# A hybrid encoder trunk: convolutions earlier into six buffers, the recurrence's odd blocks one slot later, and zero-padded keys in layer 0

## The reference

```
def bidirectional_rglru(xc, w_r, b_r, w_i, b_i, lam):
    ...
    r = jax.nn.sigmoid(jnp.einsum('bsne,dnef->dbsnf', xb, w_r...) + b_r...)
    i = jax.nn.sigmoid(jnp.einsum('bsne,dnef->dbsnf', xb, w_i...) + b_i...)
    log_a = -RG_C * r * jax.nn.softplus(-lam...)
    a = jnp.exp(log_a)
    u = jnp.sqrt(jnp.maximum(-jnp.expm1(2.0 * log_a), 0.0)) * (i * xf[None])
    h_fwd = linear_scan(a[0], u[0], reverse=False)
    h_bwd = linear_scan(a[1], u[1], reverse=True)
    return h_fwd + h_bwd

def even_mixer(h, ...):
    z = h @ w_in
    gate, xr, q, k, v = ...
    xc = lax.conv_general_dilated(xr, conv_w[:, None, :], ...) + conv_b
    y_a = bidirectional_rglru(xc, ...) * jax.nn.gelu(gate)
    y_b = dilated_mixture_attention(q, k, v).reshape(bsz, seq, B_WIDTH)
    return jnp.concatenate([y_a, y_b], axis=-1) @ w_out
```

## Time and profile before

| | |
|---|---|
| median of 3 runs | 2328.31 us (2327.73 to 2328.93) |
| the profiled execution: its own time | 2329.11 us |
| its span in the profile | 2327.3 us |
| PE busy in the span | 2273.3 us, 98% |
| DVE, ACT, POOL busy | 56%, 44%, 11% |
| mean granted clock of PE | 0.993 of full speed |

### The profile page before, as it was taken

The page is one execution under the profiler, slowest core; times in us unless marked ns, Lnnn a source line. Parts: engine busy times, 40 slices in busy tenths (PEclk is TensorE's granted clock), DMA queues, the critical chain, the costliest instruction groups (busy, mean ns, idle before and its releaser), DMA issues.

```text
span 2327.3 us, 27257 instructions
## 1 busy us (share of the span) xinstructions
PE 2273.3 (98%) x10273; PEld 1858.9 (80%) x10273; DVE 1313.6 (56%) x1308; ACT 1033.7 (44%) x1131; POOL 253.3 (11%) x243
## 2 busy tenths in 40 slices
PE   8989999899999999999999999999999999999997
PEld 6877778688888888888777777887888888888886
DVE  4567466654555555554655555676545555555555
ACT  5676444533333333343455555545434333333432
POOL 2463001400000000000340111014000000000002
PEclk9999999999999999999999999999999999999999
DMA  8545344555555555555454444555556555555552
GB/s 277 168 139 168 124 165 153 205 185 188 192 195 184 197 183 197 183 196 191 152 182 153 155 162 144 199 167 187 189 183 196 190 188 193 185 197 182 196 187 102
DMA packets 212263, 417.87 MB, mean 180 GB/s; under 512 B 12040, under 2 KB 12640, under 8 KB 211296
## 3 DMA queue, kind: packets, MB, share of 16 engines
q1 hardware_dynamic: 212192, 416.92, 54.3%
HBM read 414.79 MB, written 2.10 MB: 179 GB/s over the span
## 4 chain that ended last, share of the span: by engine, by line
issue 71%; PE 20%; POOL 4%; DVE 3%; DMA 1%; ACT 1%; SPq 0%; POOLq 0%; DVEq 0%; ACTq 0%
PE acc L937 16%; POOL yacc L1372 1%; PE tp L951 1%; DVE xs L1126 1%; DVE w_lo L1097 1%; PE sc L1018 1%; DMA gq<-in_norm_ffn_post 1%; POOL stage L1387 0%; PE sc L1023 0%; POOL small L1364 0%; PE sc L996 0%; POOL gq L1436 0%; PE pv L996 0%; POOL rot L1406 0%; PE pv L1051 0%
## 5 line engine op out<-in xcount | busy, mean ns | idle before, releaser
L1097 DVE TENSOR_TENSOR w_lo<-raw,w_hi 128x2048 fp32r<-128x2048 f32 x383 | 883.2, 2306 | 512.4 <-PE acc L937 495.3
L710 ACT ACTIVATE w_hi<-raw 128x2048 fp32r<-128x2048 f32 x383 | 734.2, 1917 | 759.5 <-PE acc L937 734.6
L937 PE MATMUL acc<-w_hi,h_hi 128*128 128x512 f32 x2240 | 888.6, 397 | 16.7 <-DVE h_lo L1102 16.7
L937 PE MATMUL acc<-w_hi,h_lo 128*128 128x512 f32 x2240 | 874.7, 390 | 0.0
L937 PE MATMUL acc<-w_lo,h_hi 128*128 128x512 f32 x2240 | 874.4, 390 | 0.0
L937 PEld LDWEIGHTS acc<-w_hi,h_hi 128*128 128x128 f32 x2240 | 422.5, 189 | 111.3 <-DVE h_lo L1102 23.4
L937 PEld LDWEIGHTS acc<-w_hi,h_lo 128*128 128x128 f32 x2240 | 421.7, 188 | 89.1
L937 PEld LDWEIGHTS acc<-w_lo,h_hi 128*128 128x128 f32 x2240 | 422.5, 189 | 84.9 <-issue 0.7
L937 PE MATMUL acc<-w_hi,y_hi 128*128 128x512 f32 x832 | 325.8, 392 | 1.9 <-DVE y_lo L1102 1.9
L937 PE MATMUL acc<-w_hi,y_lo 128*128 128x512 f32 x832 | 323.9, 389 | 0.0
L937 PE MATMUL acc<-w_lo,y_hi 128*128 128x512 f32 x832 | 323.9, 389 | 0.0
(11 more groups left out here) (142 smaller groups left out, 1058.8 us busy)
## 6 DMA issues: line engine op xcount, KB each, us to landing
raw<-in_ffn_w_gate SPq DMA_DIRECT2D x88, 1024.0 KB, 5.1
raw<-in_ffn_w_up SPq DMA_DIRECT2D x88, 1024.0 KB, 5.1
raw<-in_ffn_w_down SPq DMA_DIRECT2D x88, 1024.0 KB, 5.0
raw<-in_od_w_in SPq DMA_DIRECT2D x48, 1024.0 KB, 5.1
raw<-in_ev_w_in SPq DMA_DIRECT2D x39, 1024.0 KB, 5.2
raw<-in_ev_w_out SPq DMA_DIRECT2D x16, 1024.0 KB, 5.0
raw<-in_od_w_out SPq DMA_DIRECT2D x16, 1024.0 KB, 5.1
xs<-in_x SPq DMA_DIRECT2D x4, 512.0 KB, 9.0
```

What stands on the lines that cost most here:

```text
L710: act.activation(w_hi[u % HI][:, :, :], raw[u % RAW][:, :, :], ACT.Copy).then_inc(hi_done, 1)
L937: mm = pe.matmul(acc[n % 2][t][:, :], operand(lhs, a, k, t), w[:, k, :], start=first and k == 0 and j == 0, stop=last and k == KT - 1 and ...
L1097: dve.tensor_tensor(w_lo[u % LO][:, :, :], raw[u % RAW][:, :, :], w_hi[u % HI][:, :, :].bitcast(F32), ALU.subtract).then_inc(lo_done, 1)
```

## The change

- The eight convolutions stand in the slots 8 to 15, one each, and have six buffers instead of two (`RG_X`; four of them in a new tile `rgx`). A convolution waits for the scan of the block six before it instead of two before it.
- The gates of the blocks stand in the slots 12, 14, 17, 19, 21, 23, 25, 27 (before: 12, 13, 17, 18, 21, 22, 25, 26). Roots come three slots behind the even block's gates instead of two; the scan is three behind for even and two behind for odd blocks; outputs are a slot behind the scan. Block 7's output moves from slot 29 to slot 30.
- Layer 0's keys use layer 1's layout. POOL zeroes gx in slot 20 and kz in slot 31 of layer 0; in layer 1 only gx is left to be zeroed. ACT copies transposed keys with four instructions of 64 partitions instead of two of 128. Both score products of a head are issued together by `s0`, with 128 rows each; the wait on `s0_done` is gone. The gain load of the next block also waits for the first eight heads' scores.

```
-        slot_of = [(12, 17, 21, 25)[i // 2] + i % 2 for i in range(AT)]
+        slot_of = [(12, 17, 21, 25)[i // 2] + 2 * (i % 2) for i in range(AT)]
         for i, s in enumerate(slot_of):
-            put(s - 2, kind="rg_conv", i=i)
+            put(RG_FIRST + i, kind="rg_conv", i=i)
             put(s, kind="rg_gates", i=i)
             if i % 2 == 0:
                 for j in range(2):
-                    put(s + 2, kind="rg_root", i=i + j)
-            put(s + 2, kind="rg_scan", i=i)
+                    put(s + 3, kind="rg_root", i=i + j)
+            put(s + 3 - i % 2, kind="rg_scan", i=i)
...
-            put(s + 3, front=True, kind="rg_out", i=i)
+            put(s + 4 - i % 2, front=True, kind="rg_out", i=i)
...
-                if i >= 2:
-                    pool.wait_ge(rg_scan, RG_SCAN * (i - 2) + 2)
-                tmp, x_i = prob[:, 1, :], rg_x[i % 2]
+                if i >= RG_X:
+                    pool.wait_ge(rg_scan, RG_SCAN * (i - RG_X) + 2)
+                tmp, x_i = prob[:, 1, :], rg_x[i % RG_X]
...
+                    if task.layer == 0:
+                        for t in range(NT):
+                            mm = pe.matmul(sc[:, t, :], q[:, kt, t * P:(t + 1) * P], k[:, kt, task.i % 2, :],
+                                           start=True, stop=True)
...
-                    r, kt, t = HD * (task.i % 2), task.i // 2, j
-                    pe.matmul(sc[:, j, :], q[r:r + HD, kt, t * P:(t + 1) * P], k[r:r + HD, kt, :],
-                              start=True, stop=True).then_inc(s_done if j else s0_done, 1)
```

More of the change, by code:

```diff
@@ L54 @@
 PAR_SLOT = 6
-KEYS_SLOT = 4
+RG_FIRST = 8
+RG_X = 6
+KEYS_SLOT = ((20, 31), (4,))
 XP = T + CONV - 1
@@ L215, in mixer_slots @@
             put(PAR_SLOT + i, kind="par", i=i)
-    if layer == 1:
-        put(KEYS_SLOT, kind="zero_keys")
+    for i, s in enumerate(KEYS_SLOT[layer]):
+        put(s, kind="zero_keys", i=i)
     put(len(slots) - 12, kind="gains")
@@ L458, in trunk @@
         small = sb("small", [P, 72])
+        rgx = sb("rgx", [P, (RG_X - 2) * T])
         kz_flat = kz[:, :, :, :].rearrange("p k m t -> p (k m t)")
-        kT = [kz_flat[:, KT * T * i:KT * T * (i + 1)].rearrange("p (k t) -> p k t", k=KT) for i in range(2)]
         pre_gain, post_gain = gx[:, 0:D], gq[:, :]
@@ L466, in trunk @@
         rg_x = [gq[:, 1024 + T * i:1024 + T * (i + 1)] for i in range(2)]
+        rg_x += [rgx[:, T * i:T * (i + 1)] for i in range(RG_X - 2)]
         rg_h = gq[:, 1536:2048].rearrange("p (d t) -> p d t", d=2)
@@ L517, in trunk @@
         rope_done = sem("rope_done")
-        s0_done = sem("s0_done")
         s_done = sem("s_done")
@@ L631, in gains @@
                     sp.wait_ge(rg_out, RG_OUT * AT)
+                    sp.wait_ge(s_done, HEADS_OF_GROUP)
                 else:
@@ L766, in transposed @@
                         act.wait_ge(rg_out, RG_OUT * AT)
-                    if task.layer == 1 and task.src == "k":
+                    if task.src == "k":
                         keys_transposed(task)
                         return
-                    dst = (qT if task.src == "q" else kT)[task.g % 2][:, :, t0:t0 + P]
+                    dst = qT[task.g % 2][:, :, t0:t0 + P]
                 act.activation(dst, tp[task.e % 2][:, :, :], ACT.Copy).then_inc(tp_free[task.e % 2], 1)
@@ L775, in keys_transposed @@
                 t0, src = task.t * P, tp[task.e % 2]
-                act.wait_ge(keys_zero, 2)
+                act.wait_ge(keys_zero, 3 if task.layer else task.g + 1)
                 for m in range(2):
@@ L995, in task_of @@
                         for d in range(2):
-                            mm = pe.matmul(bank[:, d, :], rg_w[i % 2][:, 2 * j + d, :], rg_x[i % 2], start=True, stop=True)
+                            mm = pe.matmul(bank[:, d, :], rg_w[i % 2][:, 2 * j + d, :], rg_x[i % RG_X], start=True, stop=True)
                     mm.then_inc(gates_done, 1)
[L998 to L1005, removed]
+                elif task.kind == "s0":
+                    n = task.n
+                    if n > 16:
                         pe.wait_ge(exp_done, n)
@@ L1014, in task_of @@
                                 wait_event(pe, plan.ready[src, task.layer, task.g, t])
[L1015 to L1021, removed]
-                    r, kt, t = HD * (task.i % 2), task.i // 2, j
-                    pe.matmul(sc[:, j, :], q[r:r + HD, kt, t * P:(t + 1) * P], k[r:r + HD, kt, :],
-                              start=True, stop=True).then_inc(s_done if j else s0_done, 1)
+                    q, k, kt = qT[task.g % 2], keys[task.g % 2], task.i // 2
+                    if task.layer == 0:
+                        for t in range(NT):
+                            mm = pe.matmul(sc[:, t, :], q[:, kt, t * P:(t + 1) * P], k[:, kt, task.i % 2, :],
+                                           start=True, stop=True)
+                    else:
+                        t = task.i % 2
+                        mm = pe.matmul(sc[:, :, :].rearrange("p m t -> p (m t)"), q[:, kt, t * P:(t + 1) * P],
+                                       k[:, kt, :, :].rearrange("p m t -> p (m t)"), start=True, stop=True)
+                    mm.then_inc(s_done, 1)
                 elif task.kind == "pt":
@@ L1213, in scan @@
                 for d in range(2):
-                    dve.scalar_tensor_tensor(gate_i[:, d, :], gate_i[:, d, :], 1.0, rg_x[i % 2], ALU.add, ALU.mult).then_inc(rg_scan, 1)
+                    dve.scalar_tensor_tensor(gate_i[:, d, :], gate_i[:, d, :], 1.0, rg_x[i % RG_X], ALU.add, ALU.mult).then_inc(rg_scan, 1)
                 dve.wait_ge(rg_scan, k + 2)
@@ L1438, in convolve, with zero_keys @@
                         pool.wait_ge(conv_part, k + 2 * j + 1)
[L1440 to L1445, removed]
+            def zero_keys(task):
+                if task.layer == 1:
+                    pool.wait_ge(xg_done, 8 * 3)
+                elif task.i == 0:
+                    pool.wait_ge(conv_done, AT)
+                else:
+                    pool.wait_ge(rg_out, RG_OUT * AT)
+                pool.memset(keys[task.i][:, :, :, :], 0.0).then_inc(keys_zero, 1)
             def task_of(task):
@@ L1458, in task_of @@
                 elif task.kind == "zero_keys":
-                    zero_keys()
+                    zero_keys(task)
                 elif task.kind == "heads":
```

## The result

| | before | after |
|---|---|---|
| median | 2328.07 us (2327.73 to 2328.93, 4 runs) | 2308.88 us (2307.97 to 2309.23, 4 runs) |
| the profiled execution: own time, span | 2329.11, 2327.3 us | 2309.23, 2307.5 us |
| mean granted clock of PE | 0.993 | 0.997 |

The ratio is 0.9915, with a 95% interval of 0.9903 to 0.9927: 19.2 us faster. The forecast was 2307.5 us with 2302 to 2314 as its range.

The account below looks back on a forecast made before the run. PE, busy 98% of the span, was taken as the bound. Gains of 16.3 us (stalls) and 10.4 (scores) less 5.5 (new waits) make 21.2 us: 2307.5 us forecast, range 2302 to 2314.

Parts of the forecast that it names:

- The stalls: PE's gates of blocks 4 and 6 wait for POOL's convolutions, 8.15 us each; both go, 16.3 us gained.
- The scores: Layer 0's attention: score products of 128 rows save 0.65 us a slot, 16 heads, 10.4 us gained (9.3 to 11.7).
- Rival 3: Score products don't shrink, since 64-row tiles could overlap; only the stalls count: 2318.3 us, chance 5%.
- The loop of ACT and DVE: Queue work of ACT and DVE for a pair of blocks: 27.6 us, 28.7 with k0's copies, against PE's 26.2.
- The new waits: PE waits for late ACT and DVE once the stalls are gone: 5.5 us lost (3.6 to 7.1).
- Slot 20: PE waits for a lo behind block 2's gates and decay; lateness over 4.0 us becomes a wait, 0 to 2.3.
- Block 6 and the second head: ACT 4.5 us late at block 6; PE waits 3.8 us (3.6 to 4.8) from slot 28 to first pt.
- The clock: No new wait is long enough to drop PE's clock to 0.50, as behind the 5.5 us waits for POOL.
- Rival 1: The new waits don't come, because ACT and DVE overlap more than the queue sum: 2302.4 us, chance 15%.
- Rival 2: ACT and DVE later still, scans and outputs stretched in all blocks: 6 us more, 2314 us, chance 15%.
- Rival 4: PE idles 5.5 us at each of slots 20, 24, 28, 30, clock falling each time: 2335 us, chance 4%.
- Rival 5: Block 4's gates wait as long for something else, like ACT's tanh; only scores count: 2318.7 us, chance 4%.

Follow-up runs that it names:

- decay_again: The change with DVE's two decay instructions a slot later, behind w_lo, timed again on the same chip as after_again: 2301.22 us, 0.9883 of before.
- decay_later: The change with only DVE's two decay instructions of each block a slot later, behind w_lo instead of ahead of it: 2301.58 us, 0.9886 of before.
- all_three: The change with the recurrence two slots earlier, gate1's evacuation ahead of the output, and decay a slot later: 2301.25 us, 0.9886 of before.
- keys_only: The kernel before with only padded keys and joint 128-row score products for layer 0's second eight heads: 2323.74 us, 0.9982 of before.
- scores_apart: The change with 128-row score products standing apart as before, one ahead of the transposes, one behind the values: 2310.29 us, 0.9923 of before.
- after_again: The change itself, unaltered, measured a second time on the same chip as decay_again: 2309.13 us, 0.9917 of before.
- convs_only: Only the early convolutions in six buffers, with before's slots for gates, roots, scans and outputs and the old keys: 2318.98 us, 0.9964 of before.
- decay_old_table: decay_later with gates, roots, scans and outputs in the slots of the kernel before: 2307.39 us, 0.9911 of before.

## Why the prediction came out as it did

**The stalls: right, and gone.** No gates wait for POOL. The term of 16.3 us can be measured from the first matmul of slot 20 to that of slot 28; four blocks' gates lie between them in both tables, and `decay_again` waits nowhere there. Before:

```profile
137.98 0.39 PE L937 MATMUL acc<-w_hi,h_hi 128*128 128x512 f32 x1
...
206.47 0.39 PE L937 MATMUL acc<-w_hi,h_hi 128*128 128x512 f32 x1
```

and `decay_again`:

```profile
136.63 0.58 PE L941 MATMUL acc<-w_hi,h_hi 128*128 128x512 f32 x1
...
188.90 0.58 PE L941 MATMUL acc<-w_hi,h_hi 128*128 128x512 f32 x1
```

68.49 - 52.27 = 16.2 us. The kernels without any wait agree: 16.3 and 10.6 us for the scores (below) are 26.9, and 2328.13 - 26.9 = 2301.2, against 2301.58 and 2301.25 us for `decay_later` and `all_three`.

**The scores: right.** 0.65 us a head was predicted, and the slots went from 8.35 to 7.68 us, 0.67. With 0.66 for the 16 heads it is 10.6 us instead of 10.4. From the first matmul of slot 30 to that of slot 48 PE took 144.89 us in before and 134.35 in `decay_again`, 10.5 less; the half of it that `keys_only` has measured 4.5. The Trainium skill (TensorEngine Tiling (Array Packing), Key Properties) says that a change of the tiling mode drains TensorE. `scores_apart` is in line with it: with 128 rows at both places a product takes 0.43 or 0.49 us instead of 0.63, and its neighbours shrink too. A drain by itself no row here shows. Rival 3, which rested on the independence of tiles, is out.

**The loop of ACT and DVE: right in mechanism, and nearly in size.** Predicted 28.7 us from gates to gates with the key copies; in after it is 183.75 - 155.20 = 28.55 us by the table loads ahead of the gates of blocks 6 and 4:

```profile
155.20 1.28 ACT L845 ACT_TABLE_LOAD   x1
...
181.32 2.41 ACT L782 ACTIVATE gx<-tp 64x512 f32<-64x512 f32 x4
183.75 1.28 ACT L845 ACT_TABLE_LOAD   x1
```

The four key copies take 2.41 us for 1.07, 1.3 more where 1.1 was taken. With two `w_lo` less in the loop the same sum is 28.7 - 4.4 = 24.3 us, and `decay_again` took 25.22 for this pair (its tanh at 155.06 and 180.28, above). From block 2 to block 4 the loop is shorter than the 27.6 us summed up, since the output of block 1 stands ahead of the gates of block 2: 155.20 - 129.89 = 25.3 us in after (in which ACT also waits 1.64 us for a `raw` load) and 155.06 - 131.49 = 23.57 in `decay_again`. Both loops of `decay_again` are shorter than PE's 26.2 us, and so its lateness (from the end of PE's gates to ACT's table load) shrinks from block to block: 5.8, 3.3 and 2.4 us at the blocks 2, 4 and 6, where after has 6.1, 2.8 and 5.2. That is why one edit emptied all four places, the second head's too, where I had expected only the waits for `w_lo` to go.

**The new waits: the term that was mis-sized.** I took 5.5 us, with 3.6 to 7.1 as its range; in the profiled execution of after it measured 8.7. Step by step, from matmul to matmul:
- Slot 20: 0 to 2.3 us predicted, 2.23 us idle, 2.57 us lost. The lateness was put at 3 to 5.5 us. ACT began the gates of block 2 at 129.89 us, 6.1 us behind the end of PE's at 123.76. The next steps held: the lo was ready 8.6 us behind ACT's start (138.5), as predicted. So it was the start that was put too low: from the end of block 1's gates (104.79) ACT and DVE took 25.1 us, not 22.0 to 24.5. The pieces that grew are DVE's small ones, with the convolutions of blocks 6 and 7 on POOL beside them: block 0's output 2.77 us (119.70 to 122.47) for 1.70, block 1's scan 3.19 (to 125.66) for 2.71, block 1's output up to the high part 1.6 for 0.9. That POOL stretches them was the prediction's own reading of the earlier trace rows; no run takes POOL away from there.
- Block 6 and the second head: 3.6 to 4.8 us predicted, from a lateness of 4.5. It was 183.75 - 178.5 = 5.2, which by the prediction's own sum gives 5.2 + 35.5 - 36.2 = 4.5. From the end of block 7's gates to the first `pt` PE lost 4.5 us against `decay_again`, of which slot 28 has 1.7 and slot 30 0.4; the rest lies at score 1 and the first `pt`.
- The clock: "None is long enough at one place to be like rows 2." That sentence failed. In both executions of this kernel one wait of about 2 us was enough; behind the second head it cost 1.5 to 1.6 us.

Together 8.7 us: from the first matmul of slot 18 to that of slot 34 PE took 113.88 us in after and 105.22 in `decay_again`. With it the sum is 16.3 + 10.6 - 8.7 = 18.2 us, against 19.2 by the medians and 19.9 by the two profiled executions. What is missing in the sum lies ahead of slot 18. At slot 17 before takes 0.8 us more than after; it waits 0.4 us there for ACT's stage of gate1, and the three other kernels with the old table lose as much or more, so this is a small gain of the new table that the sum lacked. And before came to slot 16 at 111.05 us, after at 110.09. That 1.0 us is nothing of the change: `keys_only`, which does the same as before up to there, came at 109.69. 18.2 + 0.8 + 1.0 = 20.0. So part of the nearness of 2307.5 to 2308.88 is luck, since 3.2 us too little for the new waits met about 1.8 us that the sum didn't have.

`after_again` lost less than after on the same stretch, 111.44 - 105.22 = 6.2 us. It came to slot 16 0.3 us later than `decay_again`, and its clock fell once more near 396 us (0.72 from 395 to 401), for 0.6 us. That makes up the 7.1 us between these two profiled executions; the medians differ by 7.9.

**The rivals.** Rival 1 (no new waits, 2302.4) didn't happen in after, but `decay_later` is that case, made by an edit, and its 2301.6 us bear out the price. Rival 2 had the lateness right in kind, but too large. Rival 4 needed 6.7 us at each of four places, and the largest was 2.6 (4.1 in `after_again`, with the clock's fall behind slot 20). Rival 5 is half there in `convs_only`: with the old table, gates do wait for ACT's tanh, but 1.61 and 2.83 us instead of 5.5.

**The signs.** The first head's softmax (DVE's first L1144) starts at 216.91 us in after, 7.6 us ahead of 224.50 and not 15. The 15 went by the stalls alone and left out the waits that the same prediction has ahead of that place; `decay_again`, without them, has it at 209.22, 15.3 ahead. Full clock from 140 to 200 us holds for after and not for `after_again`. PE waits for no `raw` load, but ACT does once, for 1.64 us at 144.80.

**What failed in my later theories.** For `decay_old_table` I took 23.2 us, the loop of the new table, for a kernel with the old one. The order of the odd output and the even gates wasn't in that sum, and it is worth 29.85 - 25.22 = 4.6 us a pair.

## What to carry to other kernels

When a stall goes, write down the closed loop of each engine that had used it to catch up, in its queue's order, and compare its length with the bound engine's. Then look in that loop for an instruction that waits for another engine with work behind it that doesn't: two instructions of DVE, moved behind a `w_lo` that needed nothing of them, gave 7.9 us, more than a third of what the whole change gave. A sum of a loop holds only for the order that it was read from.

## What the runs showed that I had not expected

The clock doesn't fall at the same wait in each execution. After and `after_again` are one program, and both have the waits at slot 20 (2.23 us) and at the second head (1.74 and 1.43 us). In the first, the clock stayed at 1.00 behind slot 20 and fell behind the second head (windows above). In the second it was the other way round, as its windows show:

```profile
140.00:145.00 5.00, 5.00 (x16) 0.67 0.88 272
218.00:220.00 2.00, 1.80 (x10) 1.00 0.91 354
220.00:222.00 2.00, 2.00 (x10) 1.00 0.36 44
```

In those 5 us PE executed 16 matmuls; after had 24 there. From the first matmul of slot 20 to that of slot 22 PE took 15.00 us for 13.40, so the fall cost 1.6 us there. But these 1.6 us came back. PE was now later than `w_lo` at slot 28, where after waits 1.36 us, and had nothing to wait for:

```profile
190.08 2.28 DVE L1095 TENSOR_TENSOR w_lo<-raw,w_hi 128x2048 fp32r<-128x2048 f32 x1
...
193.23 0.58 PE L940 MATMUL acc<-w_hi,h_hi 128*128 128x512 f32 x1
```

The first `pt` started at 219.04 us in `after_again` and at 219.06 in after. ACT and DVE set that time, and a slower PE ahead of it costs nothing; the fall behind the second head has no such wait behind it, and its 1.5 us stayed.

And the longest wait of all these, 3.47 us in `decay_old_table`, left the clock at 1.00:

```profile
188.00:190.00 2.00, 2.00 (x10) 1.00 0.04 13
```

(That execution, 2305.51 us, was the fastest of four; the others took up to 2.9 us more, and no trace shows where.) So a wait of 2 us has two prices, its own or about 1.6 us more, and one profile can't tell which; the 1.6 us count in the total only where no later wait takes them up. Why the clock falls at one wait and not at another is open. Where it matters, an estimate should carry both.
